# Gated recurrence in a two-block transformer kernel: one prefix product per step, exponents as differences on VectorE, masks as predicated copies

## The reference

```python
f = lb + (1.0 - lb) * sigmoid(f_logit);  logf = log(f);  key = 1.0 - f
qf = silu(q) * dk ** -0.5
# per chunk, with a state carried from chunk to chunk
b = cumsum(lfc)                                   # over the chunk's tokens
decay = exp(where(causal, b[t] - b[s], -inf))     # per channel k
a[t, s] = sum_k qc[t, k] * kc[s, k] * decay[t, s, k]
o = (qc * exp(b)) @ state + a @ vc
state = exp(b_last) * state + (kc * exp(b_last - b)).T @ vc
```

## Time and profile before

| | |
|---|---|
| median of 3 runs | 2549.01 us (2548.95 to 2550.74) |
| span of the profiled execution | 2549.9 us |
| its own whole time | not listed beside the span |
| TensorE busy | 2496.0 us, 98% |
| VectorE busy | 1969.2 us, 77% |
| ScalarE busy | 1281.9 us, 50% |
| GpSimd busy | 265.7 us, 10% |
| recurrence in the trace | about 1430 to 1665 us |

### The profile page before, as it was taken

One profiled execution on the slowest core, in us unless ns is written; L12 is line 12 of the kernel. 1 busy time (PEld: TensorE's weight loads), 2 busy tenths in 40 slices (PEclk: granted clock), 3 DMA queues, 4 the chain that ended last, 5 costly groups with the idle time before them and its releaser, 6 DMA issues.

```text
span 2549.9 us, 32524 instructions
## 1 busy us (share of the span) xinstructions
PE 2496.0 (98%) x12435; PEld 2102.4 (82%) x12435; DVE 1969.2 (77%) x2270; ACT 1281.9 (50%) x1679; POOL 265.7 (10%) x313
## 2 busy tenths in 40 slices
PE   6999899999999999999999999999999999999999
PEld 5878787778988888888887888887898888888887
DVE  6888888897888898999867788886866566565555
ACT  4544455344554544544545664566555454453553
POOL 1000311111011112111100001350000010000000
PEclk9999999999999999999999999999999999999999
DMA  9998779987899999999857666465576676766654
GB/s 347 333 352 312 264 252 320 345 308 266 277 335 333 328 329 334 325 330 326 305 176 238 214 188 215 152 221 169 184 221 234 225 231 230 228 226 200 190 190 157
DMA packets 298811, 663.39 MB, mean 260 GB/s; under 512 B 20752, under 2 KB 21104, under 8 KB 297632
## 3 DMA queue, kind: packets, MB, share of 16 engines
q1 hardware_dynamic: 296128, 652.31, 75.3%
q0 software_dynamic: 1952, 7.30, 0.8%
q10 hardware_dynamic: 576, 1.70, 0.2%
HBM read 659.13 MB, written 2.10 MB: 259 GB/s over the span
## 4 chain that ended last, share of the span: by engine, by line
PE 83%; DVE 9%; issue 3%; DMA 2%; ACT 2%; POOL 0%; SPq 0%; DVEq 0%; ACTq 0%
PE PS L661 82%; DVE ACC L1586 3%; DVE WL L1578 2%; ACT WH L1155 1%; PE PS L664 1%; DMA RAWX<-in_w_in 1%; DVE UQ L1578 1%; DMA RAW<-in_w_in 1%; DMA RAW<-in_w_ada 0%; DMA RAW<-in_w_a_up 0%; DVE AL L1578 0%; DMA RAWX<-in_w_a_up 0%; ACT L1155 0%; DVE G L1578 0%; DVE AL L1586 0%
## 5 line engine op out<-in xcount | busy, mean ns | idle before, releaser
L1155 ACT ACTIVATE WH<-RAW 128x1024 fp32r<-128x1024 f32 x571 | 605.1, 1060 | 747.3 <-PE PS L661 608.9
L1578 DVE TENSOR_TENSOR WL<-RAW,WH 128x1024 fp32r<-128x1024 f32 x572 | 708.0, 1239 | 332.6 <-ACT WH L1155 331.0
L661 PE MATMUL PS<-WH,AH 128*128 128x512 f32 x2052 | 811.7, 396 | 10.1 <-DVE WL L1578 5.1
L661 PE MATMUL PS<-WL,AH 128*128 128x512 f32 x2052 | 800.7, 390 | 0.0
L661 PE MATMUL PS<-WH,AL 128*128 128x512 f32 x2052 | 799.2, 390 | 0.0
L661 PE MATMUL PS<-HL,WH 128*128 128x512 f32 (+1 forms) x2176 | 642.2, 383 | 0.6 <-issue 0.6
L661 PEld LDWEIGHTS PS<-WH,AH 128*128 128x128 f32 x2052 | 386.7, 188 | 94.1 <-DVE WL L1578 12.3
L661 PEld LDWEIGHTS PS<-WH,AL 128*128 128x128 f32 x2052 | 386.1, 188 | 82.2 <-DVE AL L1578 0.3
L661 PEld LDWEIGHTS PS<-WL,AH 128*128 128x128 f32 x2052 | 386.7, 188 | 77.2 <-issue 0.2
L661 PEld LDWEIGHTS PS<-HL,WL 128*128 128x128 f32 x2048 | 378.3, 188 | 85.2
L661 PE MATMUL PS<-HL,WL 128*128 128x256 f32 x2048 | 397.7, 278 | 0.0
(11 more groups left out here) (260 smaller groups left out, 1904.8 us busy)
## 6 DMA issues: line engine op xcount, KB each, us to landing
RAW<-in_w_ff SPq DMA_DIRECT2D x336, 512.0 KB, 4.6
RAW<-in_w_ada SPq DMA_DIRECT2D x280, 512.0 KB, 5.2
RAW<-in_w_in SPq DMA_DIRECT2D x194, 512.0 KB, 4.6
RAWX<-in_w_ada SPq DMA_DIRECT2D x104, 512.0 KB, 5.5
RAWY<-in_w_ff SPq DMA_DIRECT2D x96, 512.0 KB, 3.7
RAWX<-in_w_ff SPq DMA_DIRECT2D x80, 512.0 KB, 5.2
RAWX<-in_w_in SPq DMA_DIRECT2D x46, 512.0 KB, 5.1
RAW<-in_w_out SPq DMA_DIRECT2D x32, 512.0 KB, 3.6
```

Of the source, the lines that this page charges most:

```text
L661: return e.matmul(o, l, r, start=start, stop=stop, skip_group_check=True)
L1155: return e.activation(o, i, f, **kw)
L1578: return e.tensor_tensor(o, a, b, op)
```

## The change

HG0 becomes 474 and the stages are 0, 1, 2, 3, 5, 6 and 8.

- TensorE (s = 0) makes one fp32 product of log f with the triangle TRI, the prefix sums of the block, and the two transposes, all in bank 4. LFH, LFL and CT are gone; TRI is loaded alone.
- ScalarE (s = 0) copies prefix, q and k in one go (XT, now two buffers).
- VectorE (s = 1) subtracts from the prefix, for each level, the prefix in the middle of each block (a broadcast column): seven differences, and for t = 0 an eighth against the block's last.
- ScalarE (s = 2) takes the absolute value, exponentiates the last slot as it is for EX's first, and the rest with a minus sign.
- The scores (s = 5) go to bank 5 or 6 by turns. VectorE (s = 5) masks level 0 by a product and (s = 6) brings the other levels in by predicated copies straight from the bank. MP is not used.
- The output (s = 8) goes to one of two places in bank 7.

```diff
-HG0 = 475
+HG0 = 474
...
 # TensorE
-                if s == 1:
-                    e.wait_ge(s_lfh, i + 1)
...
-                    mm(PS[:, 4, :], LFH[:, :], CT[:, 0:512], True, False)
-                    e.wait_ge(s_lfl, i + 1)
-                    mm(PS[:, 4, :], LFL[:, :], CT[:, 0:512], False, True).then_inc(s_hm, 1)
-                    end = 1024 if t == 0 else 896
-                    mm(PS[:, 5, 0:end - 512], LFH[:, :], CT[:, 512:end], True, False)
-                    m = mm(PS[:, 5, 0:end - 512], LFL[:, :], CT[:, 512:end], False, t == 0)
-                    if t == 1:
-                        mm(PS[:, 5, 384:512], LFH[:, :], CT[:, 1024:1152], False, False)
-                        m = mm(PS[:, 5, 384:512], LFL[:, :], CT[:, 1024:1152], False, True)
...
+                if s == 0:
...
+                        e.wait_ge(s_hx, i)
+                    e.wait_ge(s_ln, 2 * (h // 4) + t + 1)
+                    mm(PS[:, 4, 0:128], HK[:, 1, t, hs], TRI[:, :], True, True)
+                    turn(PS[:, 4, 128:256], HG[:, 0, t, hs])
+                    turn(PS[:, 4, 256:384], HK[:, 0, t, hs]).then_inc(s_hm, 1)
+                elif s == 5:
+                    Z = PS[:, 5 + i % 2, :]
+                    e.wait_ge(s_hq, 5 * h + (2 if t == 0 else 5))
                     if i > 1:
+                        e.wait_ge(s_hv, 7 * (i - 1))
...
 # ScalarE
-                    af(EX[:, 128:640], PS[:, 4, :], ACT.Exp).then_inc(s_he, 1)
-                    e.wait_ge(s_hm, 3 * i + 2)
-                    af(EX[:, 640:1152], PS[:, 5, :], ACT.Exp).then_inc(s_he, 1)
-                    af(EX[:, 0:128], PS[:, 5, 256:384], ACT.Exp, scale=-1.0).then_inc(s_he, 1)
-                    e.wait_ge(s_hm, 3 * i + 3)
-                    af(XT[:, :], PS[:, 7, 0:256], ACT.Copy).then_inc(s_he, 1)
+                    af(XT[:, t, :], PS[:, 4, 0:384], ACT.Copy).then_inc(s_hx, 1)
+                elif s == 2:
+                    end = 1152 if t == 0 else 1024
+                    e.wait_ge(s_hd, i + 1)
+                    af(EX[:, 128:end], EX[:, 128:end], ACT.Abs).then_inc(s_ha, 1)
+                    if t == 1:
+                        af(EX[:, 1024:1152], XT[:, 1, 0:128], ACT.Exp)
+                    e.wait_ge(s_ha, 2 * i + 1)
+                    af(EX[:, 0:128], EX[:, 896:1024], ACT.Exp).then_inc(s_ha, 1)
+                    e.wait_ge(s_ha, 2 * i + 2)
+                    af(EX[:, 128:end], EX[:, 128:end], ACT.Exp, scale=-1.0).then_inc(s_he, 1)
...
 # VectorE
-                    tt(LFL[:, :], HK[:, 1, t, hs], f32(LFH[:, :]), ALU.subtract).then_inc(s_lfl, 1)
+                if s == 1:
+                    prefix = XT[:, t, 0:128]
+                    e.wait_ge(s_hx, i + 1)
+                    for l in range(LEVELS):
+                        half = 1 << l
+                        slot = (l or 7) * 128
+                        blocks = prefix.rearrange("p (n w) -> p n w", w=2 * half)
+                        middle = blocks[:, :, half - 1:half].broadcast_to([128, 64 // half, 2 * half])
+                        o = tt(EX[:, slot:slot + 128].rearrange("p (n w) -> p n w", w=2 * half), blocks, middle, ALU.subtract)
+                    if t == 0:
+                        o = tt(EX[:, 1024:1152], prefix, prefix[:, 127:128].broadcast_to([128, 128]), ALU.subtract)
+                    o.then_inc(s_hd, 1)
...
-                    tt(MP[:, 0:384], PS[:, 6, 128:512], CL[:, 128:512], ALU.mult).then_inc(s_hv, 1)
...
-                        e.wait_ge(s_hv, 8 * i + l + 1)
-                        x = second(A2[:, 0:128], l)
-                        tt(x, x, packed(MP[:, 64 * (l - 1):64 * l], l), ALU.add).then_inc(s_hv, 1)
+                        part = slice(64 + 64 * l, 128 + 64 * l)
+                        e.wait_ge(s_hv, 7 * i + l)
+                        e.copy_predicated(second(A2[:, 0:128], l), packed(CL[:, part].bitcast(I32), l),
+                                          packed(PS[:, 5 + i % 2, part], l)).then_inc(s_hv, 1)
```

More of the change, by code:

```diff
@@ L102, in constants @@
     c_pool = np.concatenate(pools, 1).astype(np.float32)
-    tm, lm = [], []
+    lm = []
     for l in range(LEVELS):
@@ L106, in constants @@
         second = (t // h) % 2 == 1
-        pre = ((t // h) * h <= s) & (s <= t)
-        suf = (t < s) & (s < (t // h + 1) * h)
-        tm.append(np.where(second, pre, suf))
         lm.append((s // (2 * h) == t // (2 * h)) & ((s // h) % 2 == 0) & second)
-    tm = tm[1:] + [tm[0], s > t, s <= t]
     lm = [(lm[0] | (s == t))] + [halves(lm[l], l)[:, :, 1, :].reshape(128, 64) for l in range(1, LEVELS)]
-    c_t = np.concatenate(tm, 1).astype(np.float32)
+    c_t = np.broadcast_to(s <= t, (128, 128)).astype(np.float32)
     c_l = np.concatenate(lm, 1).astype(np.float32)
@@ L471, in program @@
         HK = sb("HK", [128, 2, 2, 1024], F32, inner)
-        CT = sb("CT", [128, 1152], F32R, inner)
-        LFH = sb("LFH", [128, 128], F32R, inner)
-        LFL = sb("LFL", [128, 128], F32R, inner)
+        TRI = sb("TRI", [128, 128], F32, inner)
         inner.close()
@@ L585, in program @@
         s_fc, s_fr, s_fs, s_fl, s_fp = sem("f_low_part"), sem("f_relu"), sem("f_square"), sem("f_lo"), sem("f_gated")
[L586 to L589, removed]
+        s_lb, s_lbe, s_gs, s_f, s_ln = (sem("lb_difference"), sem("lb_made"), sem("gate_sigmoid"),
+                                        sem("forget"), sem("log_forget"))
+        s_hm, s_hx, s_hd, s_ha, s_he, s_hq, s_hp, s_hv, s_hk, s_hc, s_ho, s_oo = [sem("hg_" + x) for x in (
+            "prefix", "copied", "differences", "distances", "decays", "scaled", "pairs", "masked", "k7", "carry", "o", "o_copied")]
         s_an, s_trig, s_rsq, s_rms, s_rpn, s_rp = [sem("rope_" + x) for x in ("angle", "trig", "squares", "sums", "normed", "turned")]
@@ L1064, in side @@
                         turn_x(at, p - at + 3)
-                for i, s in due(p, HG0, 16, 4, (1, 4, 5, 7)):
+                for i, s in due(p, HG0, 16, 4, (0, 5, 8)):
                     hgrn(i, s)
@@ L1379, in hgrn @@
                 if s == 0:
[L1380 to L1387, removed]
[L1388 to L1394 removed]
+                    e.wait_ge(s_hm, i + 1)
+                    if i > 1:
+                        e.wait_ge(s_hq, 5 * (h - 1) + (3 if t == 0 else 5))
+                    af(XT[:, t, :], PS[:, 4, 0:384], ACT.Copy).then_inc(s_hx, 1)
[9 more added lines that the diff above has]
+                    af(EX[:, 128:end], EX[:, 128:end], ACT.Exp, scale=-1.0).then_inc(s_he, 1)
+                elif s == 5 and t == 1:
                     e.wait_ge(s_hk, h + 1)
@@ L1512, in side @@
                             log_f(half, t)
-                for i, s in due(p, HG0, 16, 4, (0, 1, 4, 7)):
+                for i, s in due(p, HG0, 16, 4, (0, 2, 5, 8)):
                     hgrn(i, s)
                 if j == HG0 + 64:
-                    e.wait_ge(s_hm, 48)
+                    e.wait_ge(s_hm, 16)
                     e.dma_start(CCN[:, 0:384], C["cc"]).then_inc(s_cc, 16)
@@ L2102, in side @@
                     tt(QK[:, 1, 0, :], QK[:, 1, 0, :], QK[:, 1, 1, :], ALU.subtract).then_inc(s_lb, 1)
-                for i, s in due(p, HG0, 16, 4, (0, 2, 4, 5)):
+                for i, s in due(p, HG0, 16, 4, (1, 3, 5, 6)):
                     hgrn(i, s)
```

72 lines of the change are left out of this document (23 added, 49 removed).

## The result

The changed kernel took 2561.64 us in the median of five runs (2557.08 to 2565.76), against 2548.95 (2547.28 to 2550.74) for the kernel before in five runs beside it: a ratio of 1.0041, with a 95% interval of 1.0031 to 1.0052. That is 12.7 us slower where 6.3 us faster was forecast, and outside the range. The profiled execution took 2565.76 us with a span of 2564.0; it is the slowest of the five, 4.1 us above their median, so its stalls are somewhat larger than those of a typical run. Over the five runs the time goes with TensorE's mean granted clock: 2557.08 us at 0.996 and 2557.56 at 0.995, 2561.64 and 2563.95 at 0.993, 2565.76 at 0.992.

The account below looks back on a forecast made before the run. TensorE's instruction count was taken to set the pace of undisturbed steps. Its work falls 12.6 us, late chains and the clock give back 6.3, so 2549.0 - 6.3 = 2542.7 us; range 2535 to 2555.

Parts of the forecast that it names:

- PE work removed and added: TensorE in the recurrence: 0.79 us less per step, 12.6 us less in all; undisturbed step becomes 13.4.
- VectorE: Differences and predicated copies raise VectorE's work per step from 11.2 to 12.1 of 13.4 us; it still fits.
- rival C: VectorE becomes the bound by the predicated copies, or by half-pace broadcast differences; slower, 2559 us; chance 0.12.
- ScalarE: ScalarE's chained part grows from 1.55 to 2.5 us (odd steps 2.6), counting only where a chain is already late.
- rival D: Abs brings a table load each way on ScalarE, making each step's chain late: 2575 us; chance 0.02.
- Where chains are late: Stalls in i = 3, i = 1, rope and the clock give back 1.6 + 1.6 + 1.3 + 1.8 = 6.3 us.
- The clock: Lower granted TensorE clock behind the stall of i = 1, as seen before at i = 3: 1.3 us given back.
- Rope: VectorE's chain from gate to scores from 1577, and the four steps that follow: 1.8 us more given back.
- Order: nothing there: Earlier HG0, stages over 8 ticks, new waits and VectorE's queue behind XT: no cost or gain.
- rival B: Gain eaten: VectorE has under 1.3 us spare per step with ada items and rope; 2549, no change; chance 0.26.
- Rival A: Full gain: late chains don't lengthen, with five ticks instead of three from prefix to scores; 2535 to 2537 us; chance 0.18.
- My test: Forecast wrong if VectorE is busy more than 13 us of an undisturbed step, or TensorE idles in every step.

Follow-up runs that it names:

- its experiment: Changed kernel with the old masks (a product into MP and six adds) in place of the predicated copies: 2562.43 us, ratio 1.0050.
- The two fills: Idle TensorE products before the KP wait: eight in i = 1, 3, 5 atop rope one tick later, 2547.00 us; five in all 16 steps of the changed kernel, 2559.11.

## Why the prediction was wrong

**PE work removed and added: right.** 13.4 was said and 13.39 came. **VectorE: right.** 12.1 was said, 12.36 and 11.67 came (mean 12.0). The two new operations by shape, 1425 to 1670:

```profile
L1552 DVE TENSOR_TENSOR EX<-XT 128x128 f32<-128x128 f32 x118 | 25.1, 281 | 0.0
...
L1944 DVE COPY_PREDICATED A<-CL,PS 128x64 f32<-128x64 int32 x84 | 20.1, 240 | 2.4
```

and one run of eight differences in its timeline:

```profile
1614.57 1.70 DVE L1552 TENSOR_TENSOR EX<-XT 128x128 f32<-128x128 f32 x8
```

Eight differences take 1.70, the 1.7 of the forecast, and six copies 1.62 instead of 1.52, so the cause that rival C names isn't there, as its experiment shows. C's time, 2559, is the nearest of all to the 2561.64 measured; that is chance. The Trainium skill (VectorE: DVE Perf Modes, The DRAIN you can't avoid) says that leaving out semaphores between operations gains nothing; by an estimate from that rule the eight would have taken 8 x 0.281 = 2.2 us. The trace disagrees. The same section also says that an operation that is not held starts earlier, which the forecast left out and the trace bears out.

**ScalarE: right.** The chained part takes 2.48 where 2.5 was said; rival D falls, since the number of table loads in the recurrence is 12 in both. At i = 1 Abs follows sigmoids and its load comes behind it (timeline, ScalarE):

```profile
1446.55 1.06 ACT L1135 ACTIVATE WH<-RAW 128x1024 fp32r<-128x1024 f32 x1 [2.35 <-PE PS L655]
1447.61 0.96 ACT L1135 ACTIVATE EX<-EX 128x896 f32<-128x896 f32 x1
1448.58 1.28 ACT L1135 ACT_TABLE_LOAD   x1
1450.09 1.28 ACT L1135 ACTIVATE EX<-EX 128x128 f32<-128x128 f32 x2
1451.39 1.28 ACT L1135 ACT_TABLE_LOAD   x1
1452.68 0.60 ACT L1135 ACTIVATE HG<-PS 128x512 f32<-128x512 f32 x1
```

The Trainium skill (ScalarE: Activation LUTs, Table sets: the hidden batching unit) says that Abs is in every set; the trace agrees. The same rows are the chain of the forecast: the sigmoid stands behind everything, and TensorE idles 2.37 (2.2 was said).

**Where chains are late: this is the step that failed**, in three of its terms.

1. The clock, put at 1.3, measured 12.0 more than before (13.7 less 1.7). I charged it at one place and for one fall of the size seen before. It fell six times, behind idles as short as 1.42 and 1.44, and cost 1.7 us or twice that. That is 10.7 of the error of 19 us. The two fills show it as a cost by itself: added work cut the time by 4.8 us on top of the moved rope, and did not raise it in the changed kernel.
2. Rope, put at 1.8, measured 6.7 more idle (7.6 from i = 10 on, 0.88 before). Two things were missing from the sum. The wait for GpSimd at SM stood 0.8 us from the chain and had no term. And a chain that is late at i = 10 does not recover: I gave the steps after it 0.1 to 0.2 each, and 0.50, 0.80, 1.42, 0.19 and 1.84 came. Moving rope alone gave 9 us back.
3. "Order: nothing there" was wrong in three places: an output waited 1.37 for the masks ahead of i = 3, the scores of i = 5 waited 1.44 behind the sines, and i = 0 waited 0.73. The differences now stand in VectorE's queue between the masks of level 0 and the copies of the others, and they were priced only as load, not as what the next low part stands behind. At i = 3 itself the stall stayed at 1.91, not 3.5; with the output's 1.37 the sum of the two is 3.28, close to the forecast, in another place.

Idle time: 5.0 more was said, 11.9 came. With the clock's 10.7 that makes 17.6 of the 19 us. Part of this is not the new form's: in the old kernel with less TensorE work 8 of some 12 us were eaten with no chain made longer. In kind this is nearest to rival B, that the gain is eaten by VectorE's small reserve, but B had neither the clock nor GpSimd and stopped at no change. Rival A needed chains that do not lengthen; the order written here does not give that. The experiment that moves the sigmoid and rope comes nearer to it and reaches 0.9966, 8.7 us where A has 12 to 14.

**My test was the wrong one.** "Wrong if VectorE is busy for more than 13 us of an undisturbed step, or if TensorE idles in every step": VectorE stays at 12 and TensorE does not idle in every step, and the kernel is slower all the same. What matters is the sum of idles long enough to bring the clock down.

**What stays open.** Idle length alone does not decide the fall: 1.42 and 1.44 brought one here, and 1.97 in the kernel with rope one tick later did not; 1.83 at i = 3 brought one with the sigmoid first and none with rope two ticks later; with five idle products in each wait 1.15 brought one and 1.69 none. One and the same kernel goes both ways: with rope one tick later four runs at a mean clock of 0.996 took 2547.54 to 2550.30 us, and six at 0.994 or 0.995 took 2553.27 to 2556.14. Of the spans' difference, some 0.4 us has no place at all, and why a stalled step keeps some of the time that an undisturbed one saves isn't known. Why GpSimd needs 1.5 us more for the same small operations isn't settled; VectorE's differences run beside them (1581.89 to 1583.58), and no run took only these away and read GpSimd's time.

## What to carry to other kernels

Work taken from the engine that sets the pace also shortens the time that every chain beside it has: before counting the gain, walk each chain from the point that releases it to the wait at its end, in the order of each queue, GpSimd's included, and write down its reserve; all reserves smaller than the cut are new stalls. In the changed kernel's profile every stall of the matrix engine from 1.42 us up was charged twice, once as idle and again by the clock (1.7 us or twice that); in its sister kernels some stalls of that size were and some were not. So a few middling stalls outweighed a cut of 12.6 us. If an order is written by hand, expect to move it with the change: one tick of rope, the sigmoid of two steps and two ticks of the sines turned 0.4% slower into 0.3% faster, of which 0.14% came to the old kernel too.

## What was not expected of the hardware

- Idle products, which add work and deliver nothing, made a kernel faster: 4.8 us for 24 products, with the granted clock at 1.00 all through the recurrence.
- A half clock can last long after one stall: behind the 2.84 of i = 10 the 3 us from 1597 to 1600 are at 0.50, and the loss there was 3.4 us, more than the stall itself.
- Predicated copies out of a score bank with an int32 mask cost little more than the adds of the same shape: 240 ns each against 226, six in a chain 1.62 against 1.52.
